# Who multiplies the last finished quadrant of the second feed-forward product by the norm weights: VectorE instead of GpSimd

## What is computed

```python
def rms_norm(x, g):
    xf = x.astype(jnp.float32)
    y = xf * lax.rsqrt(jnp.mean(xf * xf, axis=-1, keepdims=True) + EPS)
    return (y * g.astype(jnp.float32)).astype(x.dtype)
...
x = x + rms_norm(merged @ w_out[l], post_mix_g[l])
h = rms_norm(x, pre_ffn_g[l])
gt, up = jnp.split(h @ w_ffn_in[l], 2, axis=-1)
f = (jax.nn.silu(gt) * up) @ w_ffn_out[l]        # (512 x 2816) @ (2816 x 1024)
x = x + rms_norm(f, post_ffn_g[l])
```

## Time and profile before

| | |
|---|---|
| median of 3 runs | 710.19 us (709.58 to 711.63) |
| profiled execution, span from first to last instruction | 708.5 us (its own time is not given) |
| TensorE busy | 695.9 us, 98% |
| VectorE busy | 535.4 us, 76% |
| ScalarE busy | 357.4 us, 50% |
| GpSimd busy | 236.5 us, 33% |
| chain that ended last | 89% TensorE, 5% VectorE, 2% issue |

### The profile page before, as it was taken

How to read it: one execution, slowest core, us unless ns; L and a number is a source line. 1 busy time by engine, 2 the same in 40 slices (tenths; PEclk the granted TensorE clock), 3 DMA queues, 4 the chain that set the end, 5 groups by cost and what they waited for, 6 DMA issues and landing times.

```text
span 708.5 us, 11490 instructions
## 1 busy us (share of the span) xinstructions
PE 695.9 (98%) x4056; PEld 616.3 (87%) x4056; DVE 535.4 (76%) x778; ACT 357.4 (50%) x578; POOL 236.5 (33%) x213
## 2 busy tenths in 40 slices
PE   7999999999999999999999999999999999999996
PEld 6888888888888888888889999999999999888884
DVE  5438868568666656788478989878888887888997
ACT  6225544554544655234247445555455546656672
POOL 3842221122220000662123455665566550000125
PEclk9999999999999999999999999999999999999999
DMA  6168999998885213234511233223322334665563
GB/s 245 48 217 220 239 248 206 262 258 204 232 200 157 91 61 121 88 114 162 183 43 58 96 119 118 78 100 118 118 85 92 118 119 149 182 204 192 171 208 127
DMA packets 37677, 107.24 MB, mean 151 GB/s; under 512 B 4040, under 2 KB 4040, under 8 KB 37456
## 3 DMA queue, kind: packets, MB, share of 16 engines
q1 hardware_dynamic: 29648, 83.79, 34.7%
q0 software_dynamic: 8000, 23.07, 15.1%
HBM read 104.73 MB, written 25.19 MB: 183 GB/s over the span
## 4 chain that ended last, share of the span: by engine, by line
PE 89%; DVE 5%; issue 2%; ACT 1%; DMA 1%; POOL 0%; SPq 0%; DVEq 0%; POOLq 0%; ACTq 0%
PE bank L1559 28%; PE bank L1561 28%; PE bank L1560 28%; PE bank L1625 1%; DMA x_tok<-in_x_dram 1%; PE bank L1615 1%; PE bank L1616 1%; PE bank L1642 1%; DVE blk_lo L1387 1%; PE bank L1641 1%; DVE w_lo L1454 1%; DVE tm_lo L1373 0%; PE bank L1575 0%; DVE s_lo L1464 0%; ACT junk L621 0%
## 5 line engine op out<-in xcount | busy, mean ns | idle before, releaser
L1559 PE MATMUL bank<-h_hi,w_hi 128*128 128x512 f32 (+1 forms) x392 | 149.6, 382 | 0.0
L1561 PE MATMUL bank<-h_hi,w_lo 128*128 128x512 f32 (+1 forms) x392 | 147.7, 377 | 0.0
L1560 PE MATMUL bank<-h_lo,w_hi 128*128 128x512 f32 (+1 forms) x392 | 147.5, 376 | 0.0
L1001 DVE TENSOR_TENSOR w_lo<-raw,w_hi 128x1024 fp32r<-128x1024 f32 (+1 forms) x54 | 70.3, 1302 | 58.7 <-ACT w_hi L611 46.3
L1561 PEld LDWEIGHTS bank<-h_hi,w_lo 128*128 128x128 f32 x392 | 73.8, 188 | 13.7
L1559 PEld LDWEIGHTS bank<-h_hi,w_hi 128*128 128x128 f32 x392 | 73.8, 188 | 13.0 <-DVE w_lo L1001 0.4
L1560 PEld LDWEIGHTS bank<-h_lo,w_hi 128*128 128x128 f32 x392 | 73.9, 188 | 12.8
L1559 PE MATMUL bank<-tm_hi,blk_hi 128*128 128x256 f32 x240 | 67.9, 283 | 0.0
L1560 PE MATMUL bank<-tm_lo,blk_hi 128*128 128x256 f32 x240 | 67.9, 283 | 0.0
L1561 PE MATMUL bank<-tm_hi,blk_lo 128*128 128x256 f32 x240 | 67.9, 283 | 0.0
L1387 DVE TENSOR_TENSOR blk_lo<-raw_pair,blk_hi 128x512 fp32r<-128x512 f32 (+1 forms) x40 | 59.8, 1495 | 8.0 <-ACT blk_hi L860 8.0
(11 more groups left out here) (231 smaller groups left out, 1741.3 us busy)
## 6 DMA issues: line engine op xcount, KB each, us to landing
raw<-in_w_in_dram SPq DMA_DIRECT2D x42, 512.0 KB, 5.3
raw_pair<-in_w_ffn_in_dram SPq DMA_DIRECT2D x40, 512.0 KB, 4.0
comb<-in_w_ffn_out_dram POOLq DMA_DIRECT2D x30, 512.0 KB, 7.8
raw<-comb SPq DMA_DIRECT2D x20, 512.0 KB, 3.6
raw<-in_w_ffn_out_dram SPq DMA_DIRECT2D x15, 512.0 KB, 4.1
comb<-comb POOLq DMA_DIRECT2D x10, 512.0 KB, 5.3
raw<-in_w_branch_dram SPq DMA_DIRECT2D x8, 512.0 KB, 3.3
raw<-in_w_out_dram SPq DMA_DIRECT2D x8, 512.0 KB, 3.3
```

Source lines behind the costliest of these rows:

```text
L1001: dve.tensor_tensor(dst, src_hi[0], src_hi[1], ALU.subtract).then_inc(lo_done, 1)
L1559: pe.matmul(dst, a_hi, b_hi, start=start, stop=False, skip_group_check=resumed)
L1560: pe.matmul(dst, a_hi, b_lo, start=False, stop=False, skip_group_check=resumed)
L1561: return pe.matmul(dst, a_lo, b_hi, start=False, stop=stop, skip_group_check=resumed)
```

## The change

The multiplication of c22's two tiles by the second half of `gain` leaves GpSimd's list and goes into VectorE's, tile 0 behind the splits of unit 36 and tile 1 behind those of unit 37. Each waits for its tile's sum of squares and for the weights, and raises a new semaphore, `c22_gained`; VectorE's updates with c21 wait for four multiplications on GpSimd instead of six, those with c22 for the new semaphore.

```diff
@@ -286,6 +286,7 @@
+        c22_gained = sem("c22_gained")
@@ -571,10 +572,10 @@
             pool.wait_ge(gain_full, 48)
-            for i, (c, half) in enumerate(((c11, 0), (c21, 0), (c22, 1))):
+            for i, c in enumerate((c11, c21)):
                 for t in range(2):
                     pool.wait_ge(sq_done, 16 + 2 * i + t + 1)
-                    pool.tensor_tensor(c[:, t, :], c[:, t, :], gain[:, half * SEQ:(half + 1) * SEQ], ALU.mult)\
+                    pool.tensor_tensor(c[:, t, :], c[:, t, :], gain[:, 0:SEQ], ALU.mult)\
                         .then_inc(c_gained, 1)
@@ -1535,11 +1536,17 @@
                 if n == C22_MADE:
                     dve.wait_ge(p_moved, 6)
                     add_product(c22, PH_P7)
+                if n in (C22_MADE + 1, C22_MADE + 2):
+                    t = n - C22_MADE - 1
+                    dve.wait_ge(sq_done, 16 + 4 + t + 1)
+                    dve.wait_ge(gain_full, 48)
+                    dve.tensor_tensor(c22[:, t, :], c22[:, t, :], gain[:, SEQ:], ALU.mult).then_inc(c22_gained, 1)
 
             for t in range(2):
                 dve.wait_ge(rstd_done, 12 + t + 1)
-                dve.wait_ge(c_gained, 6)
+                dve.wait_ge(c_gained, 4)
                 add_x1(c21, t, 2 + t, 0)
+                dve.wait_ge(c22_gained, t + 1)
                 add_x1(c22, t, 2 + t, 1)
```

## The result

| | before | changed |
|---|---|---|
| device time, median of 20 runs each | 710.68 us (709.58 to 712.15) | 709.44 us (708.61 to 710.35) |
| ratio, 95% interval | | 0.9981 (0.9975 to 0.9987) |
| span of the profiled execution | 708.5 us | 707.5 us |

The changed kernel is 0.19% faster, that is 1.35 us (0.9 to 1.8): a real gain, and within 0.3% as forecast. A second set of runs of the changed kernel gave 0.9981 again (0.9972 to 0.9991).

The account below looks back on a forecast made before the run. VectorE was taken to bound, with TensorE waiting for unit 37's splits. Closing TensorE's hole gains 1.10 + 0.12 = 1.22 us, other terms nothing: 710.19 - 1.2 = 709.0 us, range 708.0 to 710.8.

Parts of the forecast that it names:

- What bounds: In the last 20 us TensorE waits for the splits of unit 37, so VectorE bounds; TensorE's hole is 1.10 us.
- Two stalls of 1.1 removed, two multiplications of 0.60 added: VectorE near units 36 to 38: gets back 1.11 + 1.10 = 2.21 us, takes on two 128x512 multiplications at 0.60 each.
- TensorE's hole, 1.10 + 0.12: At unit 37: the wait of 1.10 us closes and nine matmuls behind it save 0.12, 1.22 us gained.
- the slack at unit 37: Unit 37's splits let TensorE start at 695.24, but it isn't there before 695.75: 0.5 us to spare.
- the slack at unit 38: TensorE needs unit 38 at 697.11 and it is ready at 696.77, so still in time.
- The 1/rms chain at nothing: GpSimd's five small instructions for token tiles 2 and 3 start earlier, rstd there by 695.3; costed at nothing.
- The rival that the stalls are not GpSimd's: VectorE's splits stay long and it has more to do: slower by 0.67 us, 710.9 us; chance 0.04.
- The rival that GpSimd's small instructions hold VectorE: Five small instructions beside the last splits stop VectorE for their length: 710.7 to 712.5 us; chance 0.04.
- no gain: Rival: the end hangs on something unseen beside TensorE, such as the rstd chain: 710.2 us; chance 0.10.
- more than the sum: Rival: VectorE's whole relief counts, 2.2 us or more, giving 708.0 us; chance 0.07.
- the chain leaves TensorE at 692.16: Chain that ended last: from 692.16 us through VectorE's splits of units 36 and 37, releasing TensorE at 696.85; matmuls otherwise.
- The distance between device time and span: Profiled span is 1.7 us below the median of 710.19; taken as kept after the change.

Follow-up runs that it names:

- e2: Changed kernel, with GpSimd also multiplying two scratch tiles where it multiplied c22 before: ratio 1.0013 to the kernel before.
- e1: Changed kernel with c22's multiplications by the norm weights left out altogether: ratio 0.9983 to the kernel before.
- e5: Changed kernel with both c22 multiplications on VectorE ahead of the splits of unit 37: ratio 0.9988 to the kernel before.
- e6: Changed kernel with each c22 multiplication on VectorE followed by another on scratch: ratio 0.9993 to the kernel before.
- e7: Changed kernel, GpSimd also writing zeros to two scratch tiles: 12.16 us from w_lo of unit 36 to the last two x1 updates, as in the changed kernel.
- e8: Changed kernel, GpSimd also halving two scratch tiles, one input: 12.79 us from w_lo of unit 36 to the last two x1 updates, changed kernel 12.16.
- e3: Changed kernel, but GpSimd multiplies c22, only after VectorE's last split: ratio 0.9996 to the kernel before.

## Why the prediction was right

- **What bounds.** TensorE waits for VectorE's splits of unit 37, and these are late by GpSimd's multiplications: shown by e2, which brings the stalls back with scratch tiles, and by the changed kernel, where they and the wait are gone.
- **Two stalls of 1.1 removed, two multiplications of 0.60 added.** The multiplication was priced from a split of the same size and measures exactly that. Counted from w_lo of unit 36, the instructions were forecast at 1.73, 2.33, 3.46, 4.06, 4.66 and 5.26 us and start at 1.74, 2.34, 3.47, 4.08, 4.68 and 5.28.
- **The gain is TensorE's hole, 1.10 + 0.12, and not VectorE's relief.** Stretch: 1.22 us. e1 shows that VectorE's remaining 1.2 us of multiplying cost nothing, e5 that the slack at unit 37 is the 0.5 worked out, e6 that the slack at unit 38 is the 0.34 that follows from the prediction's times.
- **The 1/rms chain at nothing.** It was forecast by 695.3 and came at 695.74, which on the forecast's clock (the stretch began 0.22 later) is 0.2 late: the small instructions were stretched by more than before. The x1 updates didn't wait for it.
- **The rival that the stalls are not GpSimd's** would have given 710.9 us; e2 and the changed kernel exclude it. The Trainium skill's advice behind it (Perfetto Trace Analysis, Optimizing Scalar/DVE Operations), that it may make sense to hand work of a saturated VectorE to GpSimd, speaks for the kernel before if taken alone; its second half, that the two share an SBUF read port and that it might therefore not help, agrees with e2, e7 and e8.
- **The rival that GpSimd's small instructions hold VectorE** is excluded by the changed kernel: with one-column instructions of 1.62, 0.88 and 0.84 us beside them, VectorE's took 1.22, 0.68 and 0.68. It is GpSimd that waits. The rule that suggested it (the Trainium skill, SBUF — State Buffer, Who interferes with whom), that a VectorE instruction with two SBUF inputs contends with a GpSimd instruction that reads SBUF, is borne out at 512 columns by e2 and e8, and its exemption for a GpSimd instruction that only writes by e7. That the lock lasts for the whole instruction is not what GpSimd's records show: in e8 they are 2.03 and 1.63 us long beside a hold of 0.42.
- **The rivals of no gain and of more than the sum.** No gain is excluded by the interval (0.9975 to 0.9987) and by the end following TensorE at the same 2.15 us. More, 2.2 us or over, would be 0.9969 or less, outside the interval; e1 shows why, as VectorE's relief buys nothing beyond the hole.
- **What was misread.** By the prediction the chain leaves TensorE at 692.16, with matmuls before. In the trace of the kernel before it leaves it at 686.4, goes through ScalarE and is VectorE's from 688.00 on:

```profile
686.92 1.06 ACT w_hi L885
...
688.00 1.23 DVE w_lo L1454
```

The timelines of ScalarE and of VectorE show the same place:

```profile
686.42 0.60 ACT L986 ACTIVATE c<-bank 128x512 f32<-128x512 f32 x1 [0.73 <-PE bank L1561]
...
688.00 1.23 DVE L1454 TENSOR_TENSOR w_lo<-raw,w_hi 128x1024 fp32r<-128x1024 f32 x1 [1.29 <-ACT w_hi L885]
```

ScalarE's w_hi of unit 35 stands behind a copy of c that waits for TensorE, and VectorE idles 1.29 us for it just before the stretch. The forecast doesn't hang on this, since the gain was priced by TensorE's hole. But that idle time is a likely reason why the splits had no more lead here; no run tests it.
- **What was off.** The distance between device time and span was taken as kept, at 1.7 us; it is about 2.0 before and 1.83 now. So some 0.15 to 0.2 us of gain outside the span was missing from the sum. The forecast was 709.0 from a median of 710.19; twenty runs put the median of before at 710.68, and with that the same sum gives 709.5, against 709.44. That these two agree to 0.04 is partly luck, with that term missing and medians that move by more.

## What to carry to other kernels

An elementwise instruction on GpSimd is not free for VectorE when it reads SBUF and VectorE's own instruction has two inputs there: here 0.6 us of VectorE's work, handed to GpSimd, cost VectorE 1.1 us. Where VectorE feeds TensorE, look for VectorE records longer than their like, and see what GpSimd has beside them; but price the gain by the hole on TensorE, since two such stalls, 2.2 us, cost 1.22 in one round and 0.1 or nothing in the two others. A multiplication on VectorE costs nothing while the splits behind it are still ready in time (0.5 us of slack at unit 37); beyond that it makes a hole (e5, e6).

## What the runs showed of the hardware that I had not expected

- The hold depends on GpSimd's number of inputs from SBUF: 1.1 us for 512 columns with two (e2), 0.42 with one (e8), none with a write alone (e7). A VectorE instruction with one input from SBUF was not held (0.42 us at 433.75, before).
- It doesn't work both ways alike for small instructions: one-column GpSimd instructions beside back-to-back two-input VectorE instructions are stretched from 0.26 to as much as 1.62 us, and VectorE's don't move. In e3 that put 0.8 us on the last 1/rms, at the end of the chain; 0.2 of it came through, since VectorE was late itself.
- A hole on TensorE costs a little over its own length: the step behind it takes 0.30 or 0.31 us instead of 0.227 (before, e2, e5, e6, e8), at a granted clock of 1.00.
- The device time outside the span differs by 0.15 to 0.2 us between kernels, and went along with the number of instructions in GpSimd's list.
